# The final norm of all rows beside the last expert, the last expert's own rows mended after it

## The reference, cut to what matters

```python
def _ec_moe(h, w_router, w_gate, w_up, w_down):
    ...
    cap = max(1, CAPACITY_FACTOR * t // N_EXPERTS)
    gate, idx = lax.top_k(aff.T, cap)
    xe = tok[idx]
    hid = jax.nn.silu(jnp.einsum('ecd,edf->ecf', xe, w_gate)) * jnp.einsum('ecd,edf->ecf', xe, w_up)
    ye = jnp.einsum('ecf,efd->ecd', hid, w_down) * gate[..., None].astype(h.dtype)
    out = jnp.zeros_like(tok).at[idx.reshape(-1)].add(ye.reshape(-1, d))
    ...
# in _layer:
    return x + g2 * _ec_moe(h, w_router, w_gate, w_up, w_down)
# around it, for the prompt and for the sample:
    return _rmsnorm(x, final_norm_w)      # x * rsqrt(mean(x*x) + 1e-6) * w
```

## Time and profile before

| | us |
|---|---|
| median of 3 runs (lowest to highest) | 2866.96 (2863.33 to 2869.07) |
| span of the profiled execution | 2869.2 |
| PE busy | 2763.0 (96%) |
| DVE busy | 2155.9 (75%) |
| ACT busy | 1521.0 (53%) |
| POOL busy | 233.7 (8%) |

### The profile page before, as it was taken

How to read it: one execution, slowest core, us unless ns; L and a number is a source line. 1 busy time by engine, 2 the same in 40 slices (tenths; PEclk the granted TensorE clock), 3 DMA queues, 4 the chain that set the end, 5 groups by cost and what they waited for, 6 DMA issues and landing times.

```text
span 2869.2 us, 50738 instructions
## 1 busy us (share of the span) xinstructions
PE 2763.0 (96%) x17920; PEld 2404.1 (84%) x17920; DVE 2155.9 (75%) x4120; ACT 1521.0 (53%) x2869; POOL 233.7 (8%) x222
## 2 busy tenths in 40 slices
PE   7999889999999969999999999999999999999997
PEld 6989555666677859999999999999999999999995
DVE  4565887767765787887878878878878878778786
ACT  4443556454453345555655555555555556555554
POOL 0000421211200000000000000000000000000001
PEclk9999999999999989999999999999999999999999
DMA  7211312122146356867767768768778677677674
GB/s 278 68 64 56 124 38 77 54 106 98 58 149 224 136 175 229 260 224 249 239 226 248 250 215 254 248 221 261 224 238 268 215 247 249 224 247 252 216 235 176
DMA packets 359354, 546.67 MB, mean 191 GB/s; under 512 B 14608, under 2 KB 287760, under 8 KB 359248
## 3 DMA queue, kind: packets, MB, share of 16 engines
q1 hardware_dynamic: 352304, 520.88, 52.9%
q0 software_dynamic: 6944, 24.38, 4.2%
HBM read 493.51 MB, written 51.71 MB: 190 GB/s over the span
## 4 chain that ended last, share of the span: by engine, by line
PE 58%; DVE 3%; issue 2%; ACT 1%; DMA 1%; DVEq 0%; ACTq 0%; SPq 0%; POOL 0%; POOLq 0%
PE banks L3253 26%; PE banks L3266 14%; PE banks L3254 12%; PE banks L3226 4%; PE banks L3193 1%; DVE h_or_keys_or_sums L3110 1%; DMA slab_down<-w_down 0%; DVE hidden L3120 0%; DVE weights_low L3019 0%; ACT weights_high L2941 0%; DVE hidden_parts L3125 0%; ACT h_or_keys_or_sums L2967 0%; DVE hidden_parts L3122 0%; DVE weighted L3065 0%; DVE keys_or_w_out L3159 0%
## 5 line engine op out<-in xcount | busy, mean ns | idle before, releaser
L3253 PE MATMUL banks<-rowsT_parts,weights_high 128*128 128x384 f32 x4096 | 1210.8, 359 | 3.9 <-DVE hidden_parts L3125 2.8
L3254 PE MATMUL banks<-rowsT_parts,weights_low 128*128 128x192 f32 x4096 | 1026.3, 251 | 0.0
L3254 PEld LDWEIGHTS banks<-rowsT_parts,weights_low 128*128 128x128 f32 x4096 | 781.4, 191 | 22.3
L3253 PEld LDWEIGHTS banks<-rowsT_parts,weights_high 128*128 128x128 f32 x4096 | 769.9, 188 | 10.9 <-issue 7.8
L3019 DVE TENSOR_TENSOR weights_low<-keys_or_w_out,weights_high 128x1024 fp32r<-128x1024 f32 x512 | 603.3, 1217 | 1.4 <-ACT weights_high L2941 1.4
L2941 ACT ACTIVATE weights_high<-keys_or_w_out 128x1024 fp32r<-128x1024 f32 x512 | 523.7, 1049 | 21.9 <-PEq L2377 21.9
L3110 DVE TENSOR_TENSOR h_or_keys_or_sums<-banks,h_or_keys_or_sums 128x192 f32<-128x192 f32 x512 | 181.7, 355 | 313.8 <-ACT h_or_keys_or_sums L2967 313.7
L3266 PE MATMUL banks<-weights_high,hidden_parts 128*128 128x512 f32 x1536 | 408.0, 392 | 3.1 <-DVE hidden_parts L3125 3.0
L2967 ACT ACTIVATE h_or_keys_or_sums<-banks 128x192 f32<-128x192 f32 x512 | 165.5, 323 | 436.9 <-PE banks L3226 321.0
L3266 PEld LDWEIGHTS banks<-weights_high,hidden_parts 128*128 128x128 f32 x1536 | 282.3, 188 | 64.6 <-DVE hidden_parts L3125 8.8
L3019 DVE TENSOR_TENSOR weights_low<-slab_down,weights_high 128x1024 fp32r<-128x1024 f32 x256 | 311.6, 1217 | 0.0
...
## 6 DMA issues: line engine op xcount, KB each, us to landing
keys_or_w_out<-w_gate SPq DMA_DIRECT2D x128, 1024.0 KB, 5.2
keys_or_w_out<-w_up SPq DMA_DIRECT2D x128, 1024.0 KB, 6.8
slab_down<-w_down SPq DMA_DIRECT2D x128, 1024.0 KB, 4.9
...
```

The lines of the kernel that those rows point to most:

```text
L3253: nc.tensor.matmul(out[:, 0:2 * CT], w_hi[:, u, block], x[:, k, :], start=k == 0, stop=False)
L3254: mm = nc.tensor.matmul(out[:, 0:CT], w_lo[:, u, block], x[:, k, 0:CT], start=False, stop=k == KD - 1)
```

## The change

- The tail of all 12 tiles moves beside the last expert. A tile is loaded after expert 14's rows have been added to `residual`, into one of four places (`held`: the two buffers of gathered rows and the two of weighted results, which the last expert does not need any more). ScalarE squares it in two halves, VectorE adds the two sums, ScalarE takes the root and VectorE the reciprocal for two tiles at a time (at the units of `ROOT_AT`), and GpSimd multiplies the tile by the reciprocal and then by the norm's weight, both 128x1024. SP stores it, and its place takes the tile four later. These loads and stores are put between the weight loads of the last expert in the SP queue (`between`). The norm's weight is laid out as rows in steps 0 to 3 of the last expert, in place of steps 8 to 11; the one-hot matrices are not built.
- The 192 rows that the last expert chose are wrong in these stores. They are gathered from `residual` (`gather_left`), and at the end the last results are added to them, they are normed and scattered over the stored output (`scatter_last`), after all twelve stores have landed.
- The down products of the last slab are put in another order: the prompt's of all four units first, then the sample's left half, then its right half (`last_products`). Their number stays the same.

```diff
+ROOT_AT = (13, 18, 23, 28, 33, 38)
...
+    finals = [g for r in (1, 0) for g in range(*TILES[r])]
+    held = [t[:] for t in (*rows_of, *weighted)]
...
+                    if between is not None:
+                        between(fs, part)
+            def load_final(t):
+                if t == 0:
+                    for b in range(2):
+                        sp.wait_ge(y_out[b], (NE - 1) * 16)
+                    sp.wait_ge(x_turned, NE * TURNS)
+                if t >= 4:
+                    sp.wait_ge(tile_out[t % 4], t // 4 * 16)
+                sp.dma_start(held[t % 4], core.residual[finals[t] * P:finals[t] * P + P, :]).then_inc(tile_in[t % 4], 16)
+            def store_final(t):
+                sp.wait_ge(weighed, t + 1)
+                r = int(finals[t] >= TILES[1][0])
+                at = (finals[t] - TILES[r][0]) * P
+                sp.dma_start((io["y_prompt"], io["y_sample"])[r][0][at:at + P, :], held[t % 4]).then_inc(tile_out[t % 4], 16)
+            def between(fs, part):
+                if (fs, part) == (2, 0):
+                    load_final(0)
+                    load_final(1)
...
+                if (fs, part) == (2, 5):
+                    store_final(0)
+                if (fs, part) == (3, 0):
+                    store_final(1)
+                    load_final(4)
...
+                if (fs, part) == (3, 3):
+                    store_final(2)
+                    store_final(3)
+                    load_final(6)
+                if (fs, part) == (3, 4):
+                    load_final(7)
+                    store_final(4)
+                if (fs, part) == (3, 5):
+                    store_final(5)
+                    load_final(8)
+                    load_final(9)
-            with sp.Fori(1, NE) as e:
+            with sp.Fori(1, NE - 1) as e:
+            for fs in range(FS):
+                load(NE - 1, fs, between)
+            store_final(6)
+            store_final(7)
+            load_final(10)
+            load_final(11)
+            for t in range(8, NT):
+                store_final(t)
...
+            def gather_left():
+                wait_apart(pool, unit_lo, (NE - 1) * (FS * NU) + (FS - 1) * NU + UNITS.index((0, 3)) + 1, sem("experts_pool_turns"))
+                for b, (r, _, _) in enumerate(SPLIT):
+                    wait_apart(pool, y_out[b], (NE - 1) * 16, sem("experts_pool_turns"))
+                    nc.gpsimd.indirect_dma_start(left[b], None, core.residual, bass.IndirectOffsetOnAxis(
+                        ap=rows_in[b][:, 0:1], axis=0)).then_inc(left_in[b], 16)
+            def scatter_last(b, ready, n, tiles):
+                wait_apart(pool, ready, n, sem("experts_pool_turns"))
+                for h in range(4):
+                    wait_apart(pool, tile_out[h], tiles // 4 * 16, sem("experts_pool_turns"))
+                rows = (sample_rows[:, 0:1], rows_in[1][:, 0:1])[b]
+                nc.gpsimd.indirect_dma_start((io["y_sample"], io["y_prompt"])[b][0], bass.IndirectOffsetOnAxis(ap=rows, axis=0),
+                                             (of_sample, of_prompt)[b], None).then_inc(last_out[b], 16)
+            pool.wait_ge(row_taken, 4)
+            for t in range(NT):
+                pool.wait_ge(rstd_done, t // 2 + 1)
+                nc.gpsimd.tensor_tensor(held[t % 4], held[t % 4], rstd[:, t:t + 1].broadcast_to([P, D]), ALU.mult).then_inc(scaled, 1)
+                pool.wait_ge(scaled, t + 1)
+                nc.gpsimd.tensor_tensor(held[t % 4], held[t % 4], weight, ALU.mult).then_inc(weighed, 1)
+                if t == 9:
+                    gather_left()
+            pool.wait_ge(prompt_added, 1)
+            nc.gpsimd.tensor_tensor(prompt_by_weight, of_prompt, weight[0:CAP[0], :], ALU.mult).then_inc(prompt_weighted, 1)
+            pool.wait_ge(row_listed, 2)
+            scatter_last(1, prompt_ready, 1, NT)
+            scatter_last(0, sample_ready, 2, NT)
...
+                    for pair, root_at in enumerate(ROOT_AT):
+                        if not after and root_at - 2 <= n < root_at:
+                            final_squares(2 * pair + n - root_at + 2)
+                        if not after and n == root_at:
+                            final_root(pair)
+            def final_squares(t):
+                act.wait_ge(tile_in[t % 4], 16 * (t // 4) + 16)
+                for half in range(2):
+                    if t + half:
+                        act.wait_ge(sumsq, 2 * t + half)
+                    nc.scalar.activation(junk, held[t % 4][:, 512 * half:512 * half + 512], ACT.Square, scale=float(D) ** -0.5,
+                                         accum_out=half_sums[:, t, half:half + 1]).then_inc(sumsq, 1)
+            def final_root(pair):
+                act.wait_ge(mean_done, pair + 1)
+                nc.scalar.activation(rms[:, 2 * pair:2 * pair + 2], mean[:, 2 * pair:2 * pair + 2], ACT.Sqrt,
+                                     bias=core.eps[:, 0:1]).then_inc(root_done, 1)
...
+            act.wait_ge(prompt_mm, 1)
+            nc.scalar.activation(of_prompt, y_banks[1][CAP[0]:2 * CAP[0], :], ACT.Copy).then_inc(low_taken, 1)
+            act.wait_ge(prompt_added, 1)
+            nc.scalar.activation(last_junk[0:CAP[0], :], of_prompt, ACT.Square, scale=float(D) ** -0.5,
+                                 accum_out=last_sums[0:CAP[0], 2:3]).then_inc(last_sumsq, 1)
+            act.wait_ge(last_sumsq, 1)
+            nc.scalar.activation(last_rms[0:CAP[0], 2:3], last_sums[0:CAP[0], 2:3], ACT.Sqrt, bias=core.eps[0:CAP[0], 0:1]
+                                 ).then_inc(prompt_root, 1)
+            for half in range(2):
+                cols = slice(512 * half, 512 * half + 512)
+                act.wait_ge(sample_added, half + 1)
+                act.wait_ge(last_sumsq, half + 1)
+                nc.scalar.activation(last_junk[:, cols], of_sample[:, cols], ACT.Square, scale=float(D) ** -0.5,
+                                     accum_out=last_sums[:, half:half + 1]).then_inc(last_sumsq, 1)
+            act.wait_ge(sample_mean, 1)
+            act.wait_ge(last_sumsq, 3)
+            nc.scalar.activation(last_rms[:, 0:1], last_sums[:, 1:2], ACT.Sqrt, bias=last_mean[:, 0:1]).then_inc(sample_root, 1)
+            act.wait_ge(sample_rstd, 1)
+            nc.scalar.activation(of_sample[:, 0:512], sample_by_weight, ACT.Copy, scale=last_rstd[:, 0:1]).then_inc(sample_ready, 1)
...
+            def final_mean(pair):
+                ts = slice(2 * pair, 2 * pair + 2)
+                dve.wait_ge(sumsq, 4 * pair + 4)
+                nc.vector.tensor_tensor(mean[:, ts], half_sums[:, ts, 0], half_sums[:, ts, 1], ALU.add).then_inc(mean_done, 1)
+            def final_rstd(pair):
+                ts = slice(2 * pair, 2 * pair + 2)
+                dve.wait_ge(root_done, pair + 1)
+                nc.vector.reciprocal(rstd[:, ts], rms[:, ts]).then_inc(rstd_done, 1)
+            def finish_last():
+                fix = Order(dve, fix_order)
+                n = CAP[0]
+                gate_p, gate_s = core.gates[0:n, 64 + NE - 1:64 + NE], core.gates[:, NE - 1:NE]
+                dve.wait_ge(low_taken, 1)
+                fix.link(nc.vector.tensor_tensor(of_prompt, y_banks[1][0:n, :], of_prompt, ALU.add))
+                fix.link(nc.vector.scalar_tensor_tensor(out=of_prompt, in0=of_prompt, scalar=gate_p, in1=gain[0:n, 0, :],
+                                                        op0=ALU.mult, op1=ALU.mult))
+                dve.wait_ge(left_in[1], 16)
+                nc.vector.tensor_tensor(of_prompt, of_prompt, left[1], ALU.add).then_inc(prompt_added, 1)
+                dve.wait_ge(left_in[0], 16)
+                for half in range(2):
+                    cols = slice(512 * half, 512 * half + 512)
+                    dve.wait_ge(sample_mm, half + 1)
+                    fix.link(nc.vector.scalar_tensor_tensor(out=of_sample[:, cols], in0=y_banks[0][:, cols], scalar=gate_s,
+                                                            in1=gain[:, 1, cols], op0=ALU.mult, op1=ALU.mult))
+                    nc.vector.tensor_tensor(of_sample[:, cols], of_sample[:, cols], left[0][:, cols], ALU.add).then_inc(sample_added, 1)
+                    if half == 0:
+                        dve.wait_ge(prompt_root, 1)
+                        fix.link(nc.vector.reciprocal(last_rstd[0:n, 2:3], last_rms[0:n, 2:3]))
+                dve.wait_ge(last_sumsq, 2)
+                nc.vector.tensor_scalar(last_mean[:, 0:1], last_sums[:, 0:1], EPS, None, ALU.add).then_inc(sample_mean, 1)
+                nc.vector.tensor_tensor(sample_by_weight, of_sample[:, 0:512], weight[:, 0:512], ALU.mult)
+                dve.wait_ge(prompt_weighted, 1)
+                nc.vector.tensor_scalar(of_prompt, prompt_by_weight, last_rstd[0:n, 2:3], None, ALU.mult).then_inc(prompt_ready, 1)
+                dve.wait_ge(sample_root, 1)
+                nc.vector.reciprocal(last_rstd[:, 0:1], last_rms[:, 0:1]).then_inc(sample_rstd, 1)
```

(35 more changed lines are left out.)

170 lines of the change are left out of this document (46 added, 124 removed).

## The result

The changed kernel takes 2893.03 us (median of 4 runs), the kernel before beside it 2865.14 (4 runs): ratio 1.0095, 95% interval 1.0081 to 1.011, that is 23 to 32 us slower. The forecast was 2876, also slower, with a range up to 2892.

The account below looks back on a forecast made before the run. TensorE was taken to bound the last expert, with a 37.3 us tail behind it. Tail -21.6 and later end of products +31 gave +9.4, from 2867 to 2876 us; own range 2868 to 2885, all cases 2850 to 2892.

Parts of the forecast that it names:

- The tail: From the end of TensorE's products to the span's end: 37.3 us becomes 15.7, a gain of 21.6 us.
- The lock: Beside the last expert, GpSimd multiplies hold VectorE instructions with all inputs in SBUF: 51.2 us, less half of L3110's 7.8.
- Rival 1: Last expert: multiplies hardly hold up VectorE's splits, products end about 5 us later, time 2850; chance 0.22.
- Rival 3: Last expert: last pair or two of multiplies slip behind VectorE's last hidden part, time as before, 2867; chance 0.15.
- The failed step: Beside the last expert, VectorE waits for ScalarE's split, table load and root: 0.9 us for each of six pairs, 5.
- the slack of 0.8: End of the last expert: VectorE's last hidden part came 0.8 us before TensorE needed it, taken off the slip.
- that lead: SP queue, last expert: ScalarE takes weight halves ten units after space frees, so queue waits cost nothing, at most 5 us.
- rival 2: Last expert: all 24 multiplies at 2.37 us, waits doubled to 10 as tiles come late, time 2890; chance 0.13.
- "full, but not what decides": ScalarE beside the last expert: 34.5 us added to 35.2, busy 69.7 of 71.2, while VectorE at 98 decides.
- TensorE's clock: Last expert: if pauses let the granted clock fall from 1.00, it would be rival 2's case or worse.
- the signs named: Signs: L3019's mean over 1.22 us, TensorE under 75%, products' end E near 2863, tail 14 to 17, twelve+ table loads.

Follow-up runs that it names:

- no lock, no reload, no root: Changed kernel with GpSimd's tile multiplies on one column, tiles 4 to 11 not loaded, tiles 0 to 7 not stored, roots as copies: 2846.69 us.
- one column: Changed kernel with GpSimd's 24 tile multiplies taking one column each instead of 1024, all waits, loads and stores kept: 2864.98 us.

## Why the prediction was right and wrong

- **The tail** was right: -21.0 for -21.6, but in part by luck. Inside it the scatter lands 3.6 us after its issue, not 5.7: the row taken was for scatters that add to what is there, beside other traffic; this one only writes, beside the prompt's alone. VectorE was ready 0.7 earlier than thought, and the issue came 1.6 us after it instead of 1.1. The end of the span came 4.9 us behind the landing, not 2.0. The errors, -2.1, -0.7, +0.5 and +2.9, nearly cancel.
- **The lock** was right in its mechanism and its size in VectorE's time: 47.3 us counted (51.2 - 3.9), 41.7 measured. Taking the full length per multiply from L1107 and L3166 rather than nothing was nearer, if a little too much. The trace of before held a sign of it: the two L1107 of 316.94 stood beside two multiplies, not one (GpSimd's timeline has the line below just ahead of the one in the earlier trace rows), and their surplus of 3.41 us is 0.8 of 1.90 + 2.34 us. Rival 1 is refuted: it needed under 1.6 us per multiply, measured 1.74 (41.7/24), and in the path the multiplies cost 27.0 us, more than the tail gives back. Rival 3 did not come either: all 24 multiplies and the two gathers (x26) lie inside the stretch.

```profile
316.90 1.90 POOL L383 TENSOR_TENSOR decay_steps<-masks,steps_low 128x1024 fp32r<-128x1024 f32 x1
```

- **The failed step** is "the waits between ScalarE and VectorE for each pair of tiles ... 5". VectorE's idle time was 22.2 us. In the prediction's own sum: 94.0 + 22.2 - 71.2 = 45.0 instead of 97.7 + 5 - 71.2 - 0.8 = 30.7; waits +17.2, the lock and VectorE's own work -3.7, and the slack of 0.8 was not used up, since E comes 7.2 us after the last hidden part as before (by the prediction's own figures it was 0.7). The 0.9 us per pair priced one exchange of split, table load and root, and that came nearly as priced: the reciprocals waited 5.9 us. It left out the 9.5 us at the means, where ScalarE arrives at a tile which isn't there, and the 6.1 at the sums: it took VectorE for busy everywhere else. Taking the reloads away gave 14.2 us without the lock, 5.9 with it.
- The cause stood in the prediction twice and was priced too low. The SP queue was costed "at nothing because of that lead". The lead of ten units covers the weights (ScalarE's copies of them, L3018, waited 0.0 us), but the tiles go through the same queue, between loads that wait for VectorE's splits, and have no lead: ScalarE squares a tile as soon as its turn comes. And rival 2 named it ("ScalarE ... would reach the squares before the tile is there") with 10 us and a chance of 0.13. Rival 2 came nearest in time (2890), but by luck: it set the lock at 56.9, where 41.7 was measured, and the waits at 10, where 22.2 was. Nor did its sign come: the longest waits in the stretch were those of ScalarE's Silu for VectorE's sums (37.4 us, longest 8.5), not those for tiles (13.9, longest 7.8).
- **ScalarE "full, but not what decides"** holds (61.4 us busy for 69.7): without the roots it was busy 13 us less, and E came 4.0 us earlier. It is the order of its steps that counts, not the sum.
- **TensorE's clock**: the prediction tied a fall of it to rival 2. The same 436 products were busy for 68.98 us at 1.00 (no lock, no reload, no root), 74.62 at 0.94 (one column) and 83.26 at 0.82 (the changed kernel). So 14.3 us of TensorE's time in the stretch, booked above under lock and waits, went into the lower clock behind its pauses. What that cost the path was not measured: where VectorE sets the pace, a faster TensorE might only have waited longer.
- Of the signs named: the split's mean over 1.22 us (1.59 and 1.88), TensorE under 75% (83.26 of 116.19, 72%) and the tail at 14 to 17 came; E near 2863 did not (2871.99), nor did twelve table loads (10 in the stretch, 11 with the tail).
